# Both feed-forward products of a hybrid decoder step by one level of Strassen's scheme

## What is computed

```python
def residual_out(x, attn_o, ssm_o, w_out, norm_ffn, w_up, w_down):
    h = x + jnp.concatenate([attn_o, ssm_o], axis=-1) @ w_out
    u = rmsnorm(h, norm_ffn) @ w_up                      # 1024 -> 4096
    return h + jnp.square(jax.nn.relu(u)) @ w_down       # 4096 -> 1024
```

## Time and profile before

| | us |
|---|---|
| runs | 2045.66, 2051.59 (median), 2059.43 |
| profiled execution, span of its instructions | 2050.2 |
| first matmul of the feed-forward part | 1289.04 |
| last matmul of it ends | 2045.84 |
| end of the span less that | 4.4 |
| TensorE busy | 1947.3 |

### The profile page before, as it was taken

How to read it: one execution, slowest core, us unless ns; L and a number is a source line. 1 busy time by engine, 2 the same in 40 slices (tenths; PEclk the granted TensorE clock), 3 DMA queues, 4 the chain that set the end, 5 groups by cost and what they waited for, 6 DMA issues and landing times.

```text
span 2050.2 us, 30122 instructions
## 1 busy us (share of the span) xinstructions
PE 1947.3 (95%) x11998; PEld 1790.5 (87%) x11998; DVE 1027.6 (50%) x1366; ACT 686.0 (33%) x1170; POOL 928.1 (45%) x573
## 2 busy tenths in 40 slices
PE   8999999988888899899989999999999999999999
PEld 7999999877777888655557899999999999999998
DVE  5888812778677666489877542521221212121212
ACT  5344413666656676456640021301010101001010
POOL 4688622776676666334442234233332423333332
PEclk9999999999999999889989999999999999999999
DMA  4344435534434342789865522111111111111112
GB/s 172 140 187 169 157 122 122 130 89 104 114 79 123 101 126 73 247 292 331 281 221 204 177 95 94 42 51 42 42 42 50 41 43 49 41 51 41 51 41 95
DMA packets 118117, 239.39 MB, mean 117 GB/s; under 512 B 30187, under 2 KB 63851, under 8 KB 116348
## 3 DMA queue, kind: packets, MB, share of 16 engines
q1 hardware_dynamic: 95148, 205.72, 31.3%
q10 hardware_dynamic: 22864, 32.25, 4.8%
HBM read 187.81 MB, written 58.67 MB: 120 GB/s over the span
## 4 chain that ended last, share of the span: by engine, by line
PE 59%; DVE 11%; ACT 6%; issue 5%; DMA 1%; POOL 1%; ACTq 0%; DVEq 0%; POOLq 0%
PE wo_psa L2438 9%; PE wo_psa L2420 9%; PE wo_psb L2420 9%; PE wo_psb L2438 7%; PE dense_ps L966 6%; PE wo_psa L2260 4%; PE wo_psb L2374 2%; PE wo_psa L2374 2%; DVE att_p L1071 2%; PE att_t_ps L995 1%; ACT att_p L1165 1%; PE ssd_in L1631 1%; PE att_s_ps L984 1%; PE sa_s L1544 1%; PE sa_s L1548 1%
## 5 line engine op out<-in xcount | busy, mean ns | idle before, releaser
L913 POOL TENSOR_SCALAR att_p<-att_p,att_rden 128x128 f32<-128x128 f32 (+7 forms) x128 | 251.2, 1970 | 132.3 <-DVE att_rden L1053 132.2
L2169 POOL CAST wo_hi<-wo_raw 128x1024 fp32r<-128x1024 f32 x64 | 66.8, 1044 | 498.5 <-issue 243.0
L2534 ACT ACTIVATE r_sq<-stage 128x1056 f32<-128x1056 f32 x32 | 34.8, 1088 | 626.6 <-DVE stage L2741 626.6
L2171 POOL TENSOR_TENSOR wo_lo<-wo_raw,wo_hi 128x1024 fp32r<-128x1024 f32 x64 | 185.1, 2892 | 5.1
L1058 DVE TENSOR_TENSOR att_pTlo<-att_t_ps,att_pThi 128x512 fp32r<-128x512 f32 x192 | 106.2, 553 | 112.5 <-ACT att_pThi L1173 111.0
L2420 PE MATMUL wo_psb<-mix_split,wo_hi 128*128 128x352 f32 x768 | 144.5, 323 | 0.0
L2420 PE MATMUL wo_psa<-mix_split,wo_hi 128*128 128x352 f32 x768 | 144.2, 322 | 0.0
L1173 ACT ACTIVATE att_pThi<-att_t_ps 128x512 fp32r<-128x512 f32 x192 | 93.4, 487 | 126.8 <-PE att_t_ps L995 116.2
L966 PE MATMUL dense_ps<-u_hi,w_hi 128*128 128x352 f32 x480 | 117.3, 346 | 16.8 <-DVE conv_pre L1085 8.3
L2420 PEld LDWEIGHTS wo_psb<-mix_split,wo_hi 128*128 128x128 f32 x768 | 128.0, 188 | 0.4 <-issue 0.2
L2420 PEld LDWEIGHTS wo_psa<-mix_split,wo_hi 128*128 128x128 f32 x768 | 128.0, 188 | 0.0
(11 more groups left out here) (319 smaller groups left out, 5030.2 us busy)
## 6 DMA issues: line engine op xcount, KB each, us to landing
sa_k<-in_cache_k SPq DMA_DIRECT2D x32, 640.0 KB, 9.5
sa_v<-in_cache_v SPq DMA_DIRECT2D x40, 512.0 KB, 4.6
w_raw<-in_w_feat SPq DMA_DIRECT2D x36, 512.0 KB, 6.3
wo_raw<-in_w_up SPq DMA_DIRECT2D x32, 512.0 KB, 3.5
wo_raw<-in_w_down SPq DMA_DIRECT2D x32, 512.0 KB, 3.5
out_qk<-proj_out SPq DMA_DIRECT2D x16, 528.0 KB, 8.0
tmp_bias_rows<-tmp_table ACTq DMA_DIRECT2D x8, 1024.0 KB
att_bias<-tmp_bias_rows SPq DMA_DIRECT2D x16, 512.0 KB, 3.4
```

The costliest lines, as they stand in the source:

```text
L913: pool.tensor_scalar(slot(h, qt), slot(h, qt), rden[:, qt, :], None, ALU.mult).then_inc(normed, 1)
L2171: pool.tensor_tensor(w_lo[:, j], raw_w, w_hi[:, j].bitcast(F32), ALU.subtract).then_inc(f_split[j], 1)
```

## The change

The tokens are cut into two halves of 528 (`part(0)`, `part(1)`), taken by TensorE in two groups of 264; the inner dimension is cut into two halves; and the output features go in pairs of tiles. This gives 2x2 blocks, and each pair of output tiles is seven block products where there were eight. Their operands are the blocks and sums of blocks. An up pair is seven sets of 24 matmuls (4 row tiles, 3 split products, 2 groups), and 16 pairs make the up product. The down product goes by 8 chunks of four pairs, with seven sets of 12 matmuls in each pair. So there are 16 x 168 + 32 x 84 = 5376 matmuls of 264 columns for 4608 of 352.

- Seven split operands of the tokens, `x_set[0..6]`, are made before the first pair, out of `h` scaled by an approximate factor `x_scale` (from the sum of squares of the first five tiles; `partial_sums`, `keep_scale`, two activations Ln and Exp, `scale_x`). The exact factor `rq` is made during the first two pairs.
- `h` is then work space. It is stored to DRAM (`tmp_hid`) and loaded again before the down product.
- Sums of weights are made for each pair in `w_sums` (over the constants): four in the up product, by VectorE; in the down product two by GpSimd and two by VectorE. ScalarE now casts all operands of weights (`cast_weight`) and GpSimd makes the low parts (`split_weight`) in a ring of three sets, later six smaller ones.
- The results of an up pair are put together from seven products (`merge_*` and `relu`, VectorE; `keep_*` and `square_block`, ScalarE); sums of rows (`mix_rows`) follow, and all seven operands of the pair go to DRAM (`tmp_r_sets`). The down product loads them chunk by chunk (`load_set`), and ScalarE and VectorE split them (`cast_rows`, `split_rows`).
- In the down product VectorE adds each product to a block of `h` (`add_product`); the first product is gathered in `g_sums` over all chunks and added to three blocks in the last chunk (`add_first`).
- The feed-forward part has no hardware loop.

```diff
+KH = KD // 2
+UP_PAIRS = DFF // (2 * P)
+CHUNKS, OUT_PAIRS = 8, KD // 2
+UP_ORDER, DOWN_ORDER = (1, 5, 6, 2, 7, 3, 4), (6, 1, 5, 7, 2, 3, 4)
+NP = len(UP_ORDER)
+W_RING, W_AHEAD = 3, 6
...
+        X_AT, Z_AT, Y_AT = 6, 4, (2, 0)
...
+        def banks_of(q, m):
+            return {1: X_AT, 2: X_AT, 5: Z_AT, 3: Z_AT}.get(m, Y_AT[q % 2])
...
+            def split_operand(done, j, k0, k1, halves):
+                pool.wait_ge(s_hi, done)
+                pool.tensor_tensor(x_set[j][:, 1, k0:k1, :], halves, x_set[j][:, 0, k0:k1, :].bitcast(F32),
+                                   ALU.subtract).then_inc(s_lo_pool, 1)
...
+            def load_set(c, j):
...
+                sp.dma_start(r_half(c, j, x_raw)[:, 1], sets[:, 2 * c:2 * c + 2, DOWN_ORDER[j] - 1, :]
+                             ).then_inc(r_loaded[c % 2 * NP + j], 16)
...
+            def multiply(n, xs, ks):
...
+                pe.wait_ge(fw_split, n + 1)
+                for k in range(ks):
+                    for wi, xi in ((0, 0), (0, 1), (1, 0)):
+                        for g in range(2):
+                            mm = pe.matmul(ff_ps[:, (b + g) * 512:(b + g) * 512 + HG], ws[:, wi, k, :],
+                                           xs[:, xi, k, g * HG:(g + 1) * HG], start=(opens and k == 0 and wi == xi),
+                                           stop=(k == ks - 1 and wi == 1), skip_group_check=not opens)
+                mm.then_inc(set_done, 1)
...
+                    elif m == 6:
+                        if i == 0:
+                            pe.wait_ge(s_lo, 3)
+                            pe.wait_ge(added, KD)
...
+                    elif m == 3:
+                        pe.wait_ge(p_kept, 2 * i + 2)
+                        if i == 0:
+                            pe.wait_ge(s_lo_pool, 7)
+                    else:
+                        pe.wait_ge(merged, 5 * i + 2)
+                        if i == 0:
+                            pe.wait_ge(s_lo, 7)
+                    multiply(NP * i + j, x_set[j], KH)
...
+            for r in range(CHUNKS * OUT_PAIRS):
...
+                    else:
+                        pe.wait_ge(d_added, NP * r + {7: 1, 2: 2, 3: 3, 4: 4}[m])
+                    multiply(UP_SETS + NP * r + j, r_half(c, j, x_set), 2)
...
+                block = h[:, 2 * i + (m in (5, 7, 4)), part(int(m in (6, 5, 7, 3)))]
+                dve.tensor_tensor(two(block), two(block), out, ALU.add).then_inc(d_added, 1)
+
+            def add_first(i):
+                r = OUT_PAIRS * (CHUNKS - 1) + i
+                dve.wait_ge(d_added, NP * r + 2)
+                for t, half in ((0, 1), (1, 1), (1, 0)):
+                    block = h[:, 2 * i + t, part(half)]
+                    dve.tensor_tensor(block, block, g_sums[:, i, :], ALU.add).then_inc(g_added, 1)
...
+            for t in range(SETS - UP_SETS):
+                c, r, j = t // (NP * OUT_PAIRS), t // NP, t % NP
+                add_product(r, j)
+                if j == 1:
+                    if c == CHUNKS - 1:
+                        add_first(r % OUT_PAIRS)
+                    if r + 1 < CHUNKS * OUT_PAIRS:
+                        add_down_weights(r + 1)
+                if t == 1:
+                    for n in range(4):
+                        mix_rows(UP_PAIRS - 1, n)
+                if t % OUT_PAIRS == 2 and c + 1 < CHUNKS:
+                    split_rows(c + 1, t % (NP * OUT_PAIRS) // OUT_PAIRS)
```

More of the change, by code:

```diff
@@ L2127, in out_turned, with part, two @@
             return mixed.t_ps[:, WQ + half * P:WQ + (half + 1) * P].rearrange("p (j t) -> p j t", j=QUARTERS)
[L2129 to L2137, removed]
+        def part(half):
+            return slice(half * HN, (half + 1) * HN)
+        def two(ap):
+            return ap.rearrange("p (g c) -> p g c", g=2)
@@ new lines, in _ @@
+            for o in range(KH + 2):
+                square(o)
+            for half in range(2):
+                act.wait_ge(stat_kept, half + 1)
+                act.activation(x_scale[:, part(half)], x_scale[:, part(half)], ACT.Ln).then_inc(stat_logged, 1)
+            for half in range(2):
+                act.wait_ge(stat_logged, half + 1)
+                act.activation(x_scale[:, part(half)], x_scale[:, part(half)], ACT.Exp, scale=-0.5).then_inc(stat_rooted, 1)
+            act.wait_ge(scaled, KH)
@@ L2713, in add_part, with keep_scale @@
                                   ALU.add).then_inc(added, 1)
-            def split_x(k):
-                dve.wait_ge(x_hi_made, k + 1)
-                dve.scalar_tensor_tensor(out=m_lo[:, k, :], in0=h[:, k, :], scalar=gain_ffn[:, k:k + 1],
-                                         in1=m_hi[:, k, :].bitcast(F32), op0=ALU.mult,
-                                         op1=ALU.subtract).then_inc(x_lo_made, 1)
-            for o in range(KD - 1):
+            def keep_scale(half):
+                dve.wait_ge(stat_made, half + 1)
+                dve.tensor_scalar(two(x_scale[:, part(half)]), product(X_AT), D * EPS, None, ALU.add).then_inc(stat_kept, 1)
@@ new lines, in take_sums, with finish_scale @@
+            def take_sums(half):
+                dve.wait_ge(stat_made, half + 3)
+                dve.scalar_tensor_tensor(out=two(rq[:, part(half)]), in0=product(Y_AT[1]), scalar=D * EPS, in1=two(x_scale[:, part(half)]),
+                                         op0=ALU.add, op1=ALU.mult).then_inc(stat_kept, 1)
+            def finish_scale(half):
+                dve.wait_ge(stat_kept, half + 3)
+                dve.scalar_tensor_tensor(out=rq[:, part(half)], in0=rq[:, part(half)], scalar=1.0 / D, in1=x_scale[:, part(half)],
+                                         op0=ALU.mult, op1=ALU.mult).then_inc(q_made, 2)
```

768 lines of the change are left out of this document (615 added, 153 removed).

## The result

The changed kernel takes **1999.84 us** (median of four runs, 1998.38 to 2000.97), the kernel before 2049.03 (four runs): a ratio of 0.9755, 95% interval 0.9724 to 0.9785. The forecast was 2013 us, with 1978 to 2040 as its wide range.

A forecast was written before the change was run, and what follows sets the result against it. TensorE's pace was taken as the bound. The terms, 1290.8 + 54 + 24.5 + 287.7 + 13 + 328.7 + 9 + 3.8 = 2011.5 us, with the profile 1.4 us under the median, gave 2013 us, eight-in-ten range 1978 to 2040.

The forecast's parts named there:

- rival of hidden turns: Up product's start: VectorE and GpSimd run beside each other, first pair ends at +34 us; 1984 us in all, chance 0.20.
- output projection ends: Before the feed-forward products: the last matmul of the output projection ends at 1290.8 us, four approximate-sum matmuls added.
- end: After the last down pair: half an addition less, so 3.8 us for 4.4, with the last store the same.
- The pace: Both products: 122.3 ns per matmul of 264 columns, 657.5 us against 744.4, a gain of 86.9 us.
- rival of a fixed price: All seven products: the weight load keeps a matmul at 138.5 ns, so products gain nothing; 2100 us, chance 0.03.
- The start: First up pair: VectorE and GpSimd alternate over 59.7 us of work, ending the pair 54 us after the output projection.
- Pairs 2 and 3: Up product: 4 us added to the second pair for exact factor and relus; from the third, 20.55 us each.
- Between the products: From up to down: TensorE waits 13 us, as VectorE's first addition stands behind last merges and seven splits of rows.
- rival of late loads: Rows between products go to DRAM and back, near the highest rate at the turn; 20 us more, 2033 us, chance 0.10.
- The down product: 32 pairs of 10.27 us, 328.7 us, plus 9 us of waits: some 1.8 us a last-chunk pair, 3 us for the rest.
- rival in which this product is bound: Down product: additions out of PSUM take turns too, a pair needs 14.4 us for 10.27; 2145 us, chance 0.05.

The follow-up runs named there:

- e2_narrow: Changed kernel with each 264-token group cut into two matmuls of 132 columns in up pairs 8 to 11, three of 88 in 12 and 13; 2239.4 us, one execution.
- e5_widths: Changed kernel with matmuls of 336, 304, 288, 248, 232, 216, 200 and 176 columns, each in a single up pair; 2002.9 us, one execution.
- e1_lows_vector: Changed kernel with GpSimd's seven subtractions for sets 0, 3 and 5 of the first pair moved to VectorE; 1992.85 us, ratio 0.9721.
- e4: Changed kernel without the approximate factor: blocks are mixed from h times the gain alone, the exact factor does all scaling after the up product; 1986.74 us, ratio 0.9674.
- e7: As e4, with work that needs no late tile moved ahead of the end of the output projection; 1984.39 us, ratio 0.9668 to the kernel before.
- e8: As e7, with the low parts of sets 3 and 5 on VectorE in place of GpSimd; 1979.36 us, ratio 0.9648 to the kernel before.
- e3_turn: Changed kernel with the last three splits of rows between the products moved behind the first three additions of the down product; 2000.88 us, ratio 0.9753.
- e6_rows_twice: Changed kernel with each split of rows done twice on VectorE from the second chunk of the down product on; 2036.39 us, ratio 0.9932.

## Why the prediction was right

The time alone would not say so: 1999.84 us lies 13 from the forecast and 16 from the rival of hidden turns. The terms do:

| term | forecast | measured |
|---|---|---|
| output projection ends, us | 1290.8 | 1290.6 |
| first pair ends after it | 54 | 53.4 |
| pairs 2 and 3 beyond 20.5 each | 4 | 4.2 |
| a matmul, ns | 122.3 | 121.8 |
| waits between the products | 13 | 10.3, and 2.2 at the lower clock |
| waits in the down product | 9 | under 0.5 |
| end | 3.8 | 4.0 |
| span | 2011.5 | 1998.7 |

That the projection ends within 0.2 us of the forecast is luck, with profiled executions over 6 us apart there.

**The pace.** Right in size (87 us forecast, 89.6 measured, by 5376 x 121.8 = 654.8 against 744.4), by a rule that holds only from about 243 columns up. The rival of a fixed price has the right form: e2_narrow and e5_widths show it. Its size is 111.7 ns, not the 138.5 that would have undone the change. (I called 2100 us the result by the Trainium skill's section. By that line, 0.9 of the price at 352 columns, scaled to the 161.5 ns of the rows, 5376 matmuls would cost some 33 us more than 4608 did, so by this estimate it would be about 2133.)

**The start.** The sum of 59.7 us of work that takes turns gave +54, and TensorE's three waits came at +8.8, +27.7 and +38.6, where I had about +10, +28 and +40. e1_lows_vector shows that the sum is the cause and not VectorE's own queue: more work on VectorE, less in sum, an earlier end. That, and an end at +53.4 where hidden turns needed +34, rules out that rival (1984 us). e4, e7 and e8 take 33 us of loss down to 15.

**Pairs 2 and 3.** I had put the 4 us into the second pair; the waits are 2.0 us in the second and 1.9 in the third, each for a merge of VectorE's (L3126, L3118).

**Between the products.** I placed it rightly (VectorE's first addition behind seven splits). The size, 12.5 us lost for 13, is in part luck: my 13 were all waits, and 2.2 of the 12.5 are the lower clock behind a wait, which the forecast had nothing for. That VectorE's queue is the whole cause fell with e3_turn: the load of `h` would hold the first addition to 4 us before, and past it the rest of VectorE's work holds. So the rival of late loads is true here in part: ScalarE waited 3.9 us for rows, at 405 GB/s where I had 290. It cost TensorE nothing that can be told apart from VectorE's share. What each would cost alone stays open.

**The down product.** The term that failed: 9 us of waits, of which 1.8 us a pair for `add_first` in the last chunk (four pairs of that and the 3 us for the rest are 10.2, not the 9 that I added). They are nil. The additions are late, but a bank is wanted again only two sets later (2.9 us); I had used that room for the ordinary pairs and left it out here. e6_rows_twice shows how close it was all the same: some 0.9 us a pair of room, and 2.2 us more of splits bring the kernel to within 1% of the one before. The rival in which this product is bound (2145 us) needed additions out of PSUM to take turns, and they don't.

Of the 12.8 us between forecast and span, the down product's waits are 9, the pace over 5376 matmuls 2.7, the first pair 0.6 and the turn 0.5.

## What to carry to other kernels

When a change takes work off TensorE by giving it to VectorE and GpSimd, add up their operations with SBUF operands over both engines, at full length, leave additions out of PSUM aside, and compare the sum with TensorE's time stage by stage: in the down product there was room for 9% more here, at the start it cost 33 us. Where that sum sets the time, work between two such engines goes to the one with the lower price per element, even where its own queue is the longer. Behind a long wait of TensorE count the matmuls at the lower clock too (2.2 us at the turn here). Find the price of a matmul at the width the new tiling gives, and whether a floor lies between it and the widths you have rows of.

## What was not expected of the hardware

- A float32r matmul with its own 128x128 weight load costs 0.46 ns a column down to about 243 columns, and 111.7 ns whatever its columns below that (132 to 232, and 88 as long as the granted clock was 1.00).
- A TensorE that was busy all the time with matmuls of 88 columns had its granted clock fall from 1.00 to 0.50, and each then took 213.3 ns.
- Turns count at full length: two scalings of 2.5 us took 5.86 beside a GpSimd operation of 4.90. A scaling that reads one tile of SBUF takes turns as well (two in 4.01 us for 1.4), an addition out of PSUM doesn't.
